# VectorE in place of GpSimd makes the low parts of the next projection's weights inside the attention groups

## What is computed

```python
q, k, v = split(rmsnorm(x, g_pre_mix) @ w_in)     # one projection per head group
s = q @ k.T * 64 ** -0.5 + bias                   # ALiBi, decay or clipped relative bias
p = softmax(where(visible, s, NEG_INF))           # kind A: p0 - lam * p1, then rmsnorm of the output
x = x + rmsnorm(concat(p @ v) @ w_out, g_post_mix)
x = x + rmsnorm(square(relu(rmsnorm(x) @ w_up)) @ w_down, g_post_ffn)
```

## Time and profile before

| what | value |
|---|---|
| median of three runs | 2983.53 us |
| the profiled execution's own time | 2981.82 us |
| its span | 2980.0 us |
| TensorE products busy | 2828.4 us, 95% of the span |
| VectorE busy | 1445.7 us, 49% |
| ScalarE busy | 854.2 us, 29% |
| GpSimd busy | 664.2 us, 22% |
| low parts on GpSimd (L548) | 199, 480.7 us, 2420 ns each |
| low parts on VectorE (L1012) | 10, 12.2 us, 1216 ns each |

### The profile page before, as it was taken

The page is one execution under the profiler, slowest core; times in us unless marked ns, Lnnn a source line. Parts: engine busy times, 40 slices in busy tenths (PEclk is TensorE's granted clock), DMA queues, the critical chain, the costliest instruction groups (busy, mean ns, idle before and its releaser), DMA issues.

```text
span 2980.0 us, 49592 instructions
## 1 busy us (share of the span) xinstructions
PE 2828.4 (95%) x18736; PEld 2703.6 (91%) x18736; DVE 1445.7 (49%) x3550; ACT 854.2 (29%) x1562; POOL 664.2 (22%) x427
## 2 busy tenths in 40 slices
PE   8999999898999999999889999998899999999996
PEld 7888888798999999999878888887899999999996
DVE  6666655557333333333576565555473333333334
ACT  5444433453111111111333333335331111111121
POOL 1111100363212121212320000015431212122123
PEclk9999999998999999999989999999999999999998
DMA  5311111332111110101232111114321101010113
GB/s 187 119 59 56 68 68 67 126 139 95 36 50 35 49 56 28 56 29 56 76 124 77 62 58 58 58 66 143 131 75 50 57 28 56 28 56 35 49 36 120
DMA packets 58574, 210.32 MB, mean 71 GB/s; under 512 B 6953, under 2 KB 16561, under 8 KB 55137
## 3 DMA queue, kind: packets, MB, share of 16 engines
q1 hardware_dynamic: 54928, 173.32, 16.5%
q0 software_dynamic: 3552, 35.73, 3.0%
HBM read 163.36 MB, written 51.97 MB: 72 GB/s over the span
## 4 chain that ended last, share of the span: by engine, by line
PE 85%; DVE 6%; issue 5%; ACT 2%; POOL 1%; DMA 0%; DVEq 0%; ACTq 0%; POOLq 0%; SPq 0%
PE ps L1328 71%; PE ps L1437 4%; PE ps L1455 3%; PE ps L1402 2%; DVE XL L977 2%; PE ps L1451 1%; PE ps L1412 1%; DVE ACC L967 1%; PE ps L1414 1%; PE ps L1315 1%; PE ps L1422 1%; ACT Kh L867 1%; DVE PR L1125 1%; ACT Qh L863 1%; PE ps L1308 1%
## 5 line engine op out<-in xcount | busy, mean ns | idle before, releaser
L1328 PE MATMUL ps<-XH,WH 128*128 128x384 f32 (+1 forms) x3096 | 1029.8, 333 | 17.0 <-DVE WL L1012 11.5
L1328 PE MATMUL ps<-XL,WH 128*128 128x384 f32 (+1 forms) x3096 | 1033.1, 334 | 0.0
L1328 PE MATMUL ps<-XH,WL 128*128 128x384 f32 (+1 forms) x3096 | 1027.1, 332 | 0.0
L548 POOL TENSOR_TENSOR WL<-WS,WH 128x1024 fp32r<-128x1024 f32 x199 | 480.7, 2420 | 1771.1 <-ACT WH L687 1676.4
L1328 PE MATMUL ps<-U,WH 128*128 128x384 f32 (+1 forms) x3072 | 756.6, 330 | 0.0
L1328 PEld LDWEIGHTS ps<-XH,WH 128*128 128x128 f32 x3096 | 588.2, 190 | 25.1 <-issue 21.8
L1328 PEld LDWEIGHTS ps<-XL,WH 128*128 128x128 f32 x3096 | 588.2, 190 | 11.8 <-issue 11.8
L1328 PEld LDWEIGHTS ps<-XH,WL 128*128 128x128 f32 x3096 | 588.0, 190 | 9.4 <-issue 9.4
L1328 PEld LDWEIGHTS ps<-U,WH 128*128 128x128 f32 x3072 | 546.3, 189 | 0.0
L1328 PE MATMUL ps<-U,WL 128*128 128x384 f32 (+1 forms) x1536 | 506.1, 329 | 0.0
L687 ACT CAST WH<-WS 128x1024 fp32r<-128x1024 f32 x209 | 217.9, 1045 | 644.6 <-PE ps L1328 628.2
(11 more groups left out here) (123 smaller groups left out, 2143.5 us busy)
## 6 DMA issues: line engine op xcount, KB each, us to landing
WS<-w_in SPq DMA_DIRECT2D x209, 512.0 KB, 4.4
k_out<-KT SPq DMA_DIRECT2D x16, 672.0 KB, 3.1
x_scr<-XRES POOLq DMA_DIRECT2D x6, 1536.0 KB, 5.4
XRES<-x_scr POOLq DMA_DIRECT2D x6, 1536.0 KB, 7.2
v_out<-VT SPq DMA_DIRECT2D x16, 544.0 KB, 4.8
o_scr<-OT SPq DMA_DIRECT2D x14, 544.0 KB, 2.7
BIAS<-nc_scr SPq DMA_DIRECT2D x8, 672.0 KB, 4.8
toep_scr<-rel_scr SPq DMA_DIRECT2D x1, 5120.0 KB, 22.6
```

The source lines that it names most:

```text
L548: pool.tensor_tensor(WL[u][:, :], WS[STAGE[u]][:, :], WH[u][:, :].bitcast(f32), ALU.subtract)\
L1328: return pe.matmul(bank[:, 0:w], wt, xt, start=m == 0, stop=m == 3 * tiles - 1, skip_group_check=False)
```

## The change

In the attention groups that project (four A, three B, seven C) the three low parts move from GpSimd's program to VectorE's. VectorE makes unit 0 in slot 9 ahead of `low_queries`, unit 1 in slot 10 ahead of `low_keys`, and unit 2 at the end of the group, behind the last emptied step. GpSimd keeps the powers of the A groups; in B and C groups that project nothing is left for it, and its loop is gone. The groups that don't project, and all other sections, are as before.

```diff
+                    if sec.proj and sec.att != "A":
+                        continue
                     with runs(pool, sec) as i:
...
                         for k in range(9):
                             if sec.att == "A":
                                 rstd(k)
-                            if k == 6 and sec.proj:
-                                lo_unit(sec, i, 0, 0)
-                        if sec.proj:
-
-                            pool.wait_ge(sem["qklo"], sec.at(i, "qklo", 4))
-                            lo_unit(sec, i, 1, 1)
-                            lo_unit(sec, i, 2, 2)
-                        else:
+                        if not sec.proj:
...
+                        def low_unit(u):
+
+                            n = sec.pick(i, sec.loaded + u, sec.per["wlo"])
+                            dve.wait_ge(sem["whi"], n + 1)
+                            dve.wait_ge(sem["wlo"], n)
+                            dve.tensor_tensor(WL[u][:, :], WS[u][:, :], WH[u][:, :].bitcast(f32), ALU.subtract).then_inc(sem["wlo"], 1)
+
...
                             if sec.proj and s == 9:
+                                low_unit(0)
                                 low_queries(sec.at(i, "qkhi", 3))
                             if sec.proj and s == 10:
+                                low_unit(1)
                                 low_keys(sec.at(i, "qkhi", 4))
...
                             if sec.proj:
                                 for t in steps_in(sec.pace, s):
                                     empty_dense(t)
+                        if sec.proj:
+                            low_unit(2)
```

## The result

| | runs | median | all between |
|---|---|---|---|
| before | 11 | 2981.67 us | 2980.91 and 2986.08 |
| after | 11 | 2989.11 us | 2987.42 and 2993.01 |

The ratio is 1.0025, with a 95% interval of 1.0015 to 1.0034: slower by 7.4 us, between 4.5 and 10.1. The forecast was 6.9 us more. The median of before over all eleven runs is lower than that of the three shown earlier (2981.67 against 2983.53), and so the predicted time, 2990.4, stands 1.3 us above the measured one.

The account below looks back on a forecast made before the run. TensorE bounds the kernel, through its waits for VectorE at group boundaries. Only unit 2 between C groups costs: 6 x 0.96 + 1.14 = 6.9 us on 2983.53, giving 2990.4 us; range 2985.0 to 2993.5.

Parts of the forecast that it names:

- What bounds the kernel: TensorE's products fill 95% of the span; freeing GpSimd gains nothing; only TensorE's waits for VectorE at group boundaries count.
- 1.14 us for one low part: On VectorE, each low part pushes what stands behind it by 1.14 us if there is no hole.
- Units 0 and 1 cost nothing: Ahead of Ql (3.09 us idle) and Kl (1.70 in A, 1.26 in B and C), 1.14 us fits: cost 0.
- The thin cover: Idle time left ahead of Kl in B and C after unit 1: 0.12 us; upper bound of cost 1.0 us.
- The rival of the torn cover: Kl coming 0.3 us late at ten B and C boundaries would add 3 us: 2993.4 us; chance 0.11.
- the low parts had been late for TensorE before: If groups' first products had waited for GpSimd's units, 4.2 us would come off at 14 groups; chance 0.03.
- Unit 2 in A and B costs nothing: Group's end: B has 1.54 us idle before the first scores; in A the subtraction also fits: cost 0.
- Unit 2 between C groups: No hole ahead of the bias corners: first scores 0.96 us later at six boundaries, 1.14 at the last; 6.9 us.
- my lower bound there: Last C boundary: 1.02 us later if the chain of corners needed nothing; the whole sum would be 6.1 us.
- The released lock: A groups: VectorE's 1.37 us hold by GpSimd goes, credited nothing; rival: 5.5 us come back, 2984.9 us, chance 0.13.
- my rival: Longer TensorE idle time brings the half clock to six C boundaries: 18 us more, 3008 us; chance 0.03.
- What was to be seen: C-stretch waits for first scores grow from 0.3 to about 1.25 us at six boundaries, about 2.6 at the last.

Follow-up runs that it names:

- doubled: Changed kernel with unit 2's subtraction made twice in the C groups that project, first into a spare buffer: 3004.44 us, ratio to before 1.0076.
- the exchange: ScalarE rounds Qh ahead of weight unit 1 instead of behind it: on before 2960.16 us (0.9923), on the changed kernel 2966.83 us (0.9946).

## Why the prediction was right, and where it was off

**What bounds the kernel: right.** The change took 93 us of work off GpSimd (664.2 to 571.6) and that was worth nothing; 42 us more on VectorE would have been worth nothing as well (C's unit 2 behind the scores). What counted was one place.

**1.14 us for one low part: right.** From the start of `VT` to the first corner it is 1.13 us more, and each C interval is 1.14 longer.

**Units 0 and 1 cost nothing: right, shown.** With only C's unit 2 taken back the time is that of before. The thin cover held: `Kl` still starts 3.22 us after `Ql` and TensorE's wait for it is still 2.0. The rival of the torn cover is out. So is the one in which the low parts had been late for TensorE before: with 35 of them made on VectorE, nothing is gained.

**Unit 2 in A and B costs nothing: right, shown** by the kernel with the change in A and B alone (1.0001).

**Unit 2 between C groups: the mechanism right, one term mis-sized.** I took the chain behind the corners from the last C group, 0.12 us, and credited six boundaries with 0.18 us to spare. (The 0.12 was also measured to another instruction, a memset; from the corner to the first scores it is 0.16 there.) In the loop it isn't so: in the changed kernel TensorE's scores have been finished for over a microsecond (1698.86 + 0.32 = 1699.18), no other engine is seen to be late, and the first scores still start 0.30 us behind the last corner, as before. The 0.30 were VectorE's own need, not slack; that they ended just behind TensorE's scores in the earlier trace rows was a coincidence. So the term is 6 x 1.14 = 6.8 instead of 6 x 0.96 = 5.8. At the last boundary it was the other way: 1.01 instead of 1.14, close to my lower bound there, 1.02. Together 7.9 us, against 6.9 forecast, 7.4 measured as the difference of medians and 8.6 between the two profiled executions. Why the loop needs 0.30 us and the last group less wasn't tried; the two differ in that the loop computes its addresses and counts in registers.

**The released lock: the effect is real, its worth nothing.** 1.66 us fell to 0.29 as forecast, and the idle time ahead of `Ql` took it up. That its worth is nothing is shown by the A and B version, not only argued.

**The clock: my rival had the wrong shape.** I had it as a thing that comes or not, at 3 us a boundary and 18 in all. It came at two of six boundaries and cost nothing, as it took the place of the wait. When the wait was made 2.56 us long it came at all six, and cost 1.5 us at five of them. I had left out the case in between, in which it falls for free. What makes it fall at one boundary and not at the next like it stays open.

**What was to be seen.** "From 0.3 to about 1.25 at each of six boundaries": it was 1.43, at four, and hidden at two. Whoever had taken the sum of waits as the proof, 5.7 - 1.7 = 4.0 us, would have found half of the loss; the interval between like instructions gave all of it.

**How much a profile scatters.** The start of `Ql` in the last projection before layer 1's attention, against the profiled execution of before:

| kernel | A and B as in | at 1560 us |
|---|---|---|
| C's units 1, 2 on VectorE | before | +2.87 |
| C's unit 2 on VectorE | before | +0.86 |
| changed | changed | +1.48 |
| A and B alone | changed | -1.27 |
| C's unit 2 on GpSimd | changed | -1.73 |
| doubled | changed | -2.17 |

Kernels with the same code up to there differ by up to 3.7 us. Those with the changed A and B lie on both sides of zero, and the two others, with the code of before, stand 0.9 and 2.9 us above it. So the +1.5 us that the changed kernel's profile shows at 1560 us can't be counted as a cost of the change, and only the C intervals, which repeat six times, could be read to a tenth.

## What to carry to other kernels

When work moves to another engine, look at each place where it lands: what is the next instruction on that engine that the bottleneck engine waits for, and is there idle time ahead of it? Here 35 of 42 moved instructions were free and seven cost all of it, and standing ahead of or behind the first scores made the difference. A gap before an instruction counts as slack only if that same gap is seen smaller at the same kind of place; a like instruction outside the loop is another place. And where a bottleneck engine waits at one boundary, its feeding chain is the thing to shorten: the exchange of two statements on ScalarE was worth three times what the change cost.

## What the runs showed of the hardware

- **A half clock can replace a wait.** At two C boundaries of the changed kernel the granted clock was 0.50 (1.2 GHz) for 3.4 us, TensorE having waited 1.99 us for `Kl` just before, as it had at the four where the clock stayed at 1.00; nine products took the 1.4 us that it would have waited. The span doesn't change, TensorE's busy time grows. With a second wait of up to 2.56 us the half clock came at all six boundaries; at five it reached behind that wait and cost 1.5 us, at the sixth it lay ahead of it and was free. In the version with 20 products ahead of the transposes it fell at two boundaries and cost about 1 us at each, since there was no wait to take the place of.
- **Where the first wait was gone, the clock never fell.** In the profiles of the five kernels with the exchange TensorE doesn't wait for `Kl` between the C groups, and the granted clock is 1.00 over that whole stretch, also in the one where it waits 1.4 us for the scores at each boundary. Every fall between C groups in the other profiles stands behind a wait of 1.99 us for `Kl`, but most of these waits are followed by none: where 0.3 us of waiting for the scores came after it, the clock fell at 1 of 24 boundaries (before, A and B alone, C's unit 2 on GpSimd or behind the scores); where 1.4 us could come, at 4 of 12 (the changed kernel, C's units 1 and 2 alone); where over 2 us could come, at all 12 (doubled, C's unit 2 alone). Why isn't shown.
- **GpSimd is held by VectorE as VectorE was by GpSimd.** The power took 0.54 us by itself and 1.46 when it started 0.17 us into a low part on VectorE (334.75 against 334.58); it ended at 336.21, 0.41 after the low part, which is less than its own 0.54. The Trainium skill ("SBUF — State Buffer", Who interferes with whom) says that the port pair the two engines share is an exclusive lock, and that the order of issue decides which of them blocks. The trace agrees, in both directions: 1.66 us for VectorE's 0.29 before, 1.46 for GpSimd's 0.54 after.
- **The same subtraction on the two engines:** 2.43 us on GpSimd (mean of 157), 1.22 on VectorE (42 of them), of which 1.14 push what stands behind.
